# Fused two-block transformer forward on one core: the later modulation moved from TensorE to VectorE, its last eight slots beside the mixing output

## The reference, cut to what matters

```python
mod = (c_act @ w_mod + b_mod)[:, None, :]           # 2048 -> 6 * 2048, from one row c
mod_c = (cc_act @ w_mod + b_mod)[None, None, :]     # the same weights for the context row
sh1, sc1, gt1, sh2, sc2, gt2 = jnp.split(mod, 6, axis=-1)
csh1, csc1, cgt1, csh2, csc2, cgt2 = jnp.split(mod_c, 6, axis=-1)
h = rmsnorm(x, g_norm1) * (1 + sc1) + sh1           # 256 tokens
hc = rmsnorm(ctx, g_norm1) * (1 + csc1) + csh1      # 256 context tokens
# combined input projection (keys, queries, values, gates), bidirectional GLA and mLSTM scans
dec = jnp.einsum('btr,zrk->zbtk', glr, gla_w_lr) + gla_b_lr   # "z" below
gla_loga = jax.nn.log_sigmoid(dec) / 16
x = x + gt1 * merge_groups(...)                     # w_out: the mixing output
h2 = rmsnorm(x, g_norm2) * (1 + sc2) + sh2
x = x + gt2 * conv_ffn(h2, ...)                     # up, conv, down
# then a pooling block and an attention block, not touched here
```

## Time and profile before

| | |
|---|---|
| median of 3 runs | 2866.39 us (2863.33 to 2869.9) |
| the profiled execution | 2857.94 us |
| its span, first to last instruction | 2856.2 us |
| mean granted TensorE clock | 0.973 |
| PE, PEld, DVE, ACT busy | 2730.5, 2355.7, 2040.1, 1440.3 us |
| read from memory | 526.46 MB |

### The profile page before, as it was taken

How to read it: one execution, slowest core, us unless ns; L and a number is a source line. 1 busy time by engine, 2 the same in 40 slices (tenths; PEclk the granted TensorE clock), 3 DMA queues, 4 the chain that set the end, 5 groups by cost and what they waited for, 6 DMA issues and landing times.

```text
span 2856.2 us, 42600 instructions
## 1 busy us (share of the span) xinstructions
PE 2730.5 (96%) x16078; PEld 2355.7 (82%) x16078; DVE 2040.1 (71%) x3065; ACT 1440.3 (50%) x2001; POOL 0.2 (0%) x4
## 2 busy tenths in 40 slices
PE   7889999999989999999999999999999899999988
PEld 4457777998878888888888888889988898988877
DVE  6677886794778888887555777777654888556576
ACT  6544332444445555555444655554444654565563
POOL 0000000000000000000000000000000000000000
PEclk8999999999999999999999999999999899999989
DMA  9668756553245555555555455544555345433433
GB/s 346 225 238 328 273 221 236 177 183 105 75 161 177 191 191 190 185 189 187 187 192 193 164 191 186 182 175 178 184 188 191 134 164 179 175 136 108 176 135 131
DMA packets 104534, 530.21 MB, mean 186 GB/s; under 512 B 8240, under 2 KB 8784, under 8 KB 51296
## 3 DMA queue, kind: packets, MB, share of 16 engines
q1 hardware_dynamic: 103040, 524.32, 50.9%
q10 hardware_dynamic: 1376, 4.27, 0.4%
HBM read 526.46 MB, written 2.10 MB: 185 GB/s over the span
## 4 chain that ended last, share of the span: by engine, by line
PE 65%; DVE 6%; issue 3%; ACT 3%; ACTq 0%; DVEq 0%; DMA 0%
PE ps L1919 32%; PE ps L1920 16%; PE ps L1911 4%; PE ps L1913 4%; PE ps L1912 4%; DVE lo L1058 1%; ACT hi L499 1%; PE ps L2256 1%; DVE ws L1637 1%; PE ps L2425 1%; PE ps L2423 0%; PE ps L2261 0%; ACT L828 0%; ACT L499 0%; DVE R L1685 0%
## 5 line engine op out<-in xcount | busy, mean ns | idle before, releaser
L1058 DVE TENSOR_TENSOR lo<-raw,hi 128x1024 fp32r<-128x1024 f32 x700 | 845.0, 1223 | 475.4 <-ACT hi L499 471.9
L499 ACT ACTIVATE hi<-raw 128x1024 fp32r<-128x1024 f32 x700 | 732.3, 1056 | 613.7 <-PE ps L1920 545.8
L1919 PE MATMUL ps<-x,hi 128*128 128x512 f32 x1376 | 479.8, 395 | 7.3 <-DVE x L1504 7.2
L1920 PE MATMUL ps<-x,lo 128*128 128x256 f32 x1376 | 382.2, 278 | 0.0
L1919 PE MATMUL ps<-y,hi 128*128 128x512 f32 x1024 | 363.2, 399 | 3.6 <-DVE y L1889 3.6
L1919 PE MATMUL ps<-xp,hi 128*128 128x512 f32 x1024 | 361.0, 396 | 5.7 <-DVE lo L1058 3.9
L533 ACT ACTIVATE hi<-raw 128x1024 fp32r<-128x1024 f32 x194 | 200.4, 1055 | 316.3 <-PE ps L1910 137.9
L1138 DVE TENSOR_TENSOR lo<-raw,hi 128x1024 fp32r<-128x1024 f32 x194 | 230.9, 1221 | 124.6 <-ACT hi L533 124.2
L1919 PEld LDWEIGHTS ps<-x,hi 128*128 128x128 f32 x1376 | 259.0, 188 | 69.1 <-issue 8.2
L1920 PE MATMUL ps<-y,lo 128*128 128x256 f32 x1024 | 288.5, 282 | 0.0
L1920 PE MATMUL ps<-xp,lo 128*128 128x256 f32 x1024 | 287.8, 281 | 0.0
(11 more groups left out here) (384 smaller groups left out, 5075.8 us busy)
## 6 DMA issues: line engine op xcount, KB each, us to landing
raw<-in_weights SPq DMA_DIRECT2D x491, 1024.0 KB, 4.8
xf<-in_xt SPq DMA_DIRECT2D x8, 512.0 KB, 9.0
raw<-in_weights SPq DMA_DIRECT2D x4, 768.0 KB, 4.2
R<-in_xt ACTq DMA_DIRECT2D x1, 2048.0 KB, 8.1
out<-R SPq DMA_DIRECT2D x1, 2048.0 KB, 6.3
maskn<-in_maskn ACTq DMA_DIRECT2D x1, 512.0 KB, 3.7
ptr<-in_pt ACTq DMA_DIRECT2D x2, 256.0 KB, 3.8
vec<-in_vec ACTq DMA_DIRECT2D x1, 411.5 KB, 4.6
```

The source lines that it names most:

```text
L499: act.activation(HI[p % PAIR][:, c], RAW[p % RING][:, c], ACT.Copy).then_inc(hi_ready, 1)
L1058: dve.tensor_tensor(LO[p % PAIR][:, c], RAW[p % RING][:, c], HI[p % PAIR][:, c].bitcast(F32), ALU.subtract).then_inc(lo_ready, 1)
L1919: pe.matmul(o, h, pair[:, :, k, :], start=start, stop=False, **kw)
L1920: return pe.matmul(o[:, 0, :], l, pair[:, 0, k, :], start=False, stop=stop, **kw)
```

## The change

It has four parts.

1. `SUMMED` now begins with group 4: 56 slots (32 to 87) go through VectorE's multiply-and-add in the front, none of the later modulation is split. The sums of four slots go to TensorE as before, now 14 times in the front, each with its own bias addition (`later_modulation(g)`).
2. The last eight slots (88 to 95, `FINAL`) are no longer in `UNITS`: they are loaded by ScalarE's queue to two buffers of their own (`wlast`) and summed on VectorE in turns 3, 5, 6, 8, 9, 11, 12 and 14 of the mixing output; TensorE takes their two column sums behind the sum of squares.
3. The list of units is new. The slots of `MODS[3]` all stand ahead of `("key4", 2)`; behind it come `("key", 5, 0)`, the last quarter `("key4", 3)` and `("key", 5, 1)`. The operand of quarter 3 is made behind the first half of `key4 2` (`operand_made(3)`, `operand_hi(3)`, `operand_rest(3)`).
4. ScalarE makes z and |z| out of PSUM (Identity and Abs with bias), and the squares of the residual in the mixing output.

```diff
-LATER = MODS[4]
-SUMMED = [u for m in MODS[5:] for u in m]
+SUMMED = [u for m in MODS[4:] for u in m][:56]
+FINAL = [u for u in MODS[7] if u not in SUMMED]
+FINAL_TURNS = (3, 5, 6, 8, 9, 11, 12, 14)
...
-UNITS += whole(("key4", 1), ("lr_key", 0)) + modulation_of(MODS[2][6:] + MODS[3][:6]) + whole(("key4", 2))
-UNITS += modulation_of(MODS[3][6:] + LATER[:6]) + whole(("key4", 3))
...
+UNITS += whole(("key4", 1), ("lr_key", 0)) + modulation_of(MODS[2][6:] + MODS[3]) + whole(("key4", 2)) + [("key", 5, 0)]
+UNITS += whole(("key4", 3)) + [("key", 5, 1)] + modulation_of(SUMMED[:1])
+_b = 1
+for _entry in [("lr_key", 1), ("key", 6), ("key", 7)]:
+    UNITS += [(*_entry, 0)] + modulation_of(SUMMED[_b:_b + 1]) + [(*_entry, 1)] + modulation_of(SUMMED[_b + 1:_b + 2])
...
-    if _entry in (("query", 5), ("query", 7), ("gate", 1), ("gate", 3), ("gate", 6), ("gate", 8), ("gate", 11), ("gate", 13)):
+    if _entry in (("query", 4), ("query", 5), ("query", 7), ("gate", 1), ("gate", 2), ("gate", 4), ("gate", 5), ("gate", 7), ("gate", 8), ("gate", 10),
+                  ("gate", 11), ("gate", 12), ("gate", 13)):
...
+            def operand_hi(r):
+
+                for s in range(2):
+                    act.wait_ge(sem("operand_made"), reached("made", "x1", 2 * r + s + 1))
+                    act.activation(xs(xh, s, r), xs(xf, s, r), ACT.Copy).then_inc(sem("operand_hi"), 1)
...
+                    if n == AT["value", 2 * m] + 1:
...
+                            act.activation(cum[:, m * 1024 + a * 512:m * 1024 + (a + 1) * 512], PS[4 + a][:, :], ACT.Identity,
+                                           bias=v("lr_b", 2 * m + a)).then_inc(sem("dec_abs"), 1)
+                            act.activation(soft[:, c], PS[4 + a][:, :], ACT.Abs, bias=v("lr_b", 2 * m + a)).then_inc(sem("dec_abs"), 1)
...
+            def n2_square(b):
+
+                act.wait_ge(evacuated, EVAC["mix_out"] + b + 1)
+                if b >= 2:
+                    act.wait_ge(sem("square_steps"), reached("steps", "n2", b - 1))
+                act.activation((tmpx, tmpx2)[b % 2][:, :], blk(R, b), ACT.Square).then_inc(sem("squares_ready"), 1)
+
+            def load_final(i):
+
+                if i >= 2:
+                    act.wait_ge(sem("mod_summed"), 4 * (NSUM + i) - 4)
+                act.dma_start(wlast[i % 2][:, :], A["weights"][MOD_AT + FINAL[i]]).then_inc(sem(f"last_loaded{i % 2}"), 16)
...
             for u in range(16):
                 split("mix_out", u // RING, u % RING)
+                if u - 1 in FINAL_TURNS[:6]:
+                    load_final(FINAL_TURNS.index(u - 1) + 2)
                 if u:
+                    n2_square(u - 1)
                     n2_gain(u - 1)
...
+            def later_modulation(g):
+
+                dve.wait_ge(sem("sums_taken"), g + 1)
+                j = 32 + 4 * g
+                dve.tensor_tensor(mview[:, j:j + 4, 0], PS[7][:, 4 * g:4 * g + 4], v("b_mod", j, 4), ALU.add).then_inc(sem("mods_ready"), 1)
...
+            for u in range(16):
+                split("mix_out", u // RING, u % RING)
...
-                accumulate(Steps(dve, sem("square_steps"), reached("steps", "n2") + 2 * u), blk(R, u), tmpx)
+                if u:
+                    n2_sum(u - 1)
+                if u in FINAL_TURNS:
+                    i = FINAL_TURNS.index(u)
+                    dve.wait_ge(sem(f"last_loaded{i % 2}"), 16 * (i // 2 + 1))
+                    multiplied_sum(NSUM + i, FINAL[i], wlast[i % 2], range(4))
+            n2_sum(15)
...
+                if AT[kind, k] - 1 in LAST and half == (kind != "key4"):
+                    turn_rows(LAST.index(AT[kind, k] - 1))
...
             sum_squares("n2", "steps")
+            column_sums(14)
+            column_sums(15)
```

More of the change, by code:

```diff
@@ L405, in sums_of @@
         def sums_of(g):
-            return wsum[g % 2 + (0 if GROUP_ENDS[g] < AT["value", 10] else 2)]
+            return wsum[4 + g % 2 if g >= len(GROUP_ENDS) else g % 2 + (0 if GROUP_ENDS[g] < AT["value", 10] else 2)]
         def cum_of(d, c):
@@ L556, in _ @@
                 n = AT[kind, k]
-                if half and n in LAST[:5]:
+                if half and n in LAST:
                     r = LAST.index(n)
@@ L562, in _ @@
                     act.activation(mrows[:, :], PS[6 + r % 2][0:16, :], ACT.Copy).then_inc(sem("mod_rows"), 1)
+                if (kind, k, half) == ("key4", 2, 1):
+                    operand_hi(3)
                 if UNITS[u] in HALF:
@@ L587, in _ @@
                     act.wait_ge(halves_used, HALF[UNITS[u]] + 1)
-                    key_out(k, k - 5)
+                    key_out(k, 6 if k == 5 else k - 5)
                 if kind == "query":
@@ L1227, in scan, with operand_made, operand_rest @@
                 own.wait()
+            def operand_made(r):
+                modulation(r)
+                for s in range(2):
+                    gains(s, 16, s, "g1", 4 * r, 4)
+                own.wait()
+                for s in range(2):
+                    for b in range(4 * r, 4 * r + 4):
+                        f = s * KD + b
+                        ins = dve.tensor_scalar(blk(xf, f), blk(xf, f), amod[:, f:f + 1], mview[:, b, s:s + 1], ALU.mult, ALU.add)
+                    ins.then_inc(sem("operand_made"), 1)
+            def operand_rest(r):
+                for s in range(2):
+                    dve.wait_ge(sem("operand_hi"), reached("hi", "x1", 2 * r + s + 1))
+                    dve.tensor_tensor(xs(xl, s, r), xs(xf, s, r), xs(xh, s, r).bitcast(F32), ALU.subtract).then_inc(sem("operand_rest"), 1)
             dve.memset(ones[:, :], 1.0).then_inc(sem("ones_ready"), 1)
@@ L1249, in _ @@
                     level_arg(m)
+                if (kind, k, half) == ("key4", 2, 1):
+                    operand_made(3)
+                    operand_rest(3)
                 if UNITS[u] in HALF:
@@ L1286, in _ @@
                     z = cum[:, m * 1024:(m + 1) * 1024]
-                    if n == AT["value", 2 * m] + 1:
-                        for a in range(2):
-                            dve.wait_ge(sem("dec_z"), 2 * m + a + 1)
-                            own.done(dve.tensor_scalar(z[:, a * 512:(a + 1) * 512], PS[4 + a][:, :], v("lr_b", 2 * m + a), None, ALU.add))
-                        own.wait()
-                        dve.scalar_tensor_tensor(soft[:, :], z, -1.0, z, ALU.mult, ALU.max).then_inc(sem("dec_abs"), 1)
                     if n == AT["value", 2 * m + 1] + 1:
```

165 lines of the change are left out of this document (76 added, 89 removed).

## The result

The changed kernel took 2838.91 us, median of four runs (2821.49 to 2842.42), the kernel before 2867.91 (2863.33 to 2869.9). The ratio is 0.9895, 95% interval 0.9855 to 0.9935: 29 us faster, or 1%. The profiled execution took 2836.49 us, its span 2834.7. The forecast was 2830.6. Its direction and its outer range (2821 to 2846) held, its own narrower range (2823 to 2837) missed by 2 us. One of its sentences was wrong by 9 us, and some 3 us more than forecast, won elsewhere, hid a part of that; 2 us of these are granted clock and not the change.

The account below looks back on a forecast made before the run. TensorE, busy 2730 of 2856 us, was taken as the bound. Terms 45.1 - 0.95 - 5.0 - 1.7 - 1.6 = 35.8 us won, off the 2866.4 median, gave 2830.6; own range 2823 to 2837, outer 2821 to 2846.

Parts of the forecast that it names:

- Front: Up to the first value slot: it starts at 252.3 instead of 295.4 us, 43.1 won, 45.1 with clock given back.
- the rival of a front that gives back: Keys and queries: late transfers or low parts cost four waits, 8 us, leaving 28 won, 2839 us; chance 0.11.
- the 1.2 taken: Front, from `key4 2` to the first value slot: 1.2 us counted for the clock.
- Values: Value stage: three more sums, 9 us of VectorE, hide in its idle time; one more group of column sums costs 0.95.
- the sum: Whole kernel: 45.1 - 0.95 - 5.0 - 1.7 - 1.6 = 35.8 us won.
- The walk: Gates: VectorE's order followed gate by gate gives 6.7 us of TensorE waits ahead of scores; stage ends 5.0 us later.
- VectorE as the bound to the full price of 12.1 us: Rival for gates and mixing output: they lose 12.1 and 12 us, leaving 20 won, 2846 us; chance 0.13.
- The pairs: Mixing output: sums in consecutive turns (5, 6; 8, 9; 11, 12) make waits of 0.6 us each, 1.7 in all.
- The tail: End of mixing output: TensorE's wait ahead of the n2 sum is 5.9 us instead of 4.24, costing 1.6.
- the two queues: Rival in mixing output: eight transfers on ScalarE's queue compete with weights, 23 us if none hid, 2854 us; chance 0.05.
- the slower rival: Mixing output: VectorE waits for late `wlast` loads; at 19 us a load, 42 lost, 2873 us; chance 0.03.
- The last two column sums and their bias are beside the norm.: Behind the mixing output: these were taken as hidden beside the norm, with no cost in the sum.

Follow-up runs that it names:

- a0: The changed kernel run once more with no edit; 2835.13 us, ratio 0.9907.
- e7: On top of e1, four of the gates' sums moved to value slots where VectorE was idle, some value sums shifted; 2822.14 us, ratio 0.9849.
- e6: The changed kernel with no half of key quarter 5 ahead of `key4 3`, both halves behind it; 2835.93 us, ratio 0.9879.
- e9: The same kernel as e7 run once more; 2814.41 us, ratio 0.9828.
- e2: The changed kernel with four modulation sums moved from the gates into value slots 8, 10, 12 and 14; 2844.01 us, ratio 0.9919.
- e4: The kernel before with only z and |z| of the decay moved to ScalarE; 2864.52 us, ratio 0.9992.
- e5: The kernel before with only the squares of n2 moved to ScalarE; 2863.33 us, ratio 0.9984.
- e10: As e7, with the eight sums beside the mixing output in turns 1, 3, 4, 6, 8, 9, 11 and 13; 2825.15 us.
- e1: The changed kernel with both last column sums placed ahead of both bias additions; 2828.07 us, ratio 0.987.

## Why the prediction was right, and where it was wrong

**Front.** Right. `key4 2` at 158.33 (158.0 forecast), `key4 3` at 177.3 without a wait (177.6; operand at 173.3, margin 4.0 instead of 5.5), first value slot at 251.18 (252.3). No wait for `raw` in the queries, so the rival of a front that gives back is out. The clock cost 1.7 us for the 1.2 taken (granted 0.77 from 157.7 to 165.0 us, 7.3 x 0.23). The 1.2 was the author's estimate and no run shows it: behind the same wait of 2.40 us the runs showed 1.7 us by that clock, as in a0 and e7, or nothing (1.00 over the same 7.3 us, e6 and e9). (1.75 slots of 1.05 MB at 361 GB/s are 5.1 us and not 4.9; it changes nothing.)

**Values.** Right within what can be told: the sum has 2.0 us of clock back and 0.95 lost, 1.05 us won (the 2.0 are 7 x 0.28, by the 0.72 granted behind the wait of 3.50 us; the changed kernel has 1.00 over the 7.2 us from 251.0), and first value slot to first gate took 245.4 us (246.5 in a0) for 245.9, in a stage that differs by over 1 us between executions. The reason was too coarse: the three sums were hidden, four more in the same stage were not (e2), since slots 9 to 12 have no room left. A new wait of 1.8 us for a bias addition was not in the sum; those for V fell from 11.9 to 10.4.

**Gates.** The walk forecast waits of 6.7 us for `qk` (its seven terms add up to 6.8) and the trace has 5.5, ahead of the scores of the very gates it named: 0.3, 0.2, 0.1, 1.3, 1.0, 1.4 and 1.3 us at 2, 5, 7, 8, 11, 12 and 13, forecast 0.4, 1.1, 0.1, 1.6, 0.4, 1.6 and 1.6. The stage is 6.3 us longer than before where 5.0 were forecast; 4.3 are waits and 0.95 the column sums, about 1 us is open. Mechanism shown by e2 and e7: with six sums the waits are 1.0. VectorE as the bound to the full price of 12.1 us is out.

**Mixing output.** Off in size. The pairs were 1.7 us in the sum and cost 0.1 at most, with no wait. The additions behind a pair end 5.0 to 5.4 us after the slot's end, where the prediction had 6.1, so the bank was free just in time: at 758.76, for TensorE's slot 9 at 758.90, a margin of 0.14 us, where every turn of before had 2.1. The stage is 1.1 us longer, 0.85 of it in its first slot (7.31 us for 6.46, granted clock 0.75 for 0.86). That is not the change's doing: the same slot took 7.60 us in e4, which has the mixing output of before, and 6.33 in e2, which has the changed one. The tail was 1.6 us in the sum and is 0.9, for the reason given (VectorE's queue; e5, e10); ScalarE's square, 0.5 in the sum, took 0.40 us. No wait for `wlast`: its loads landed in 4.8 us (median), so neither the two queues nor the slower rival came about.

**The step that failed** is "The last two column sums and their bias are beside the norm." They were put down at nothing; they cost 9.0 us (e1). TensorE's side was looked at (0.95 us a group, with a wait for x2 to hide in) and the bias's duration (0.15 us), but not that the second group of sums waits for the first group's bias, and that this stands on VectorE behind 14 us of x2. Up to the n2 sum 38.5 us were won where the sum had 35.8. Of the 2.7 more, 2.0 are the granted clock between the gates and the mixing output, for which the sum has no term: that is luck. Without the missed 9.0 the median would have been near 2830, which is the forecast, and with it it is 2838.9. How near the medians come is luck in part too, since each is of four executions and those of the changed kernel are 21 us apart.

## What to carry to other kernels

A tiny instruction is as late as the queue it stands in (here 0.15 us of bias behind 14 us of x2, 12.93 us of waiting): for each edit "beside" something, write down what its waits need and what is ahead of that on its engine. A stage's mean idle share is no room (VectorE idled 42.5 of 155 us in the values before, but 0.8 of 20 around slots 10 and 11 of the changed kernel); look at windows of a slot or two before moving work in. Before a gain of 1 or 2 us is put down to an edit, look at the granted clock of that stretch in both profiles (0.93 and 0.96 were 2.0 us apart here). And compare waits and starts inside the profiles, not two totals, when stages can run at two periods, as here at 346.7 and 353.3 ns a pair.

## What the runs showed of the hardware

A stretch of matmul pairs (512 and 256 columns) at a granted clock of 1.00, with no wait, ran at one of two periods, 346.7 or 353.3 ns, and kept it to the end of a stage in most cases: 1376 pairs of `up` would be 9.2 us apart by that, and the stage was 7.4 and 7.9 us longer in the changed kernel's first profile than before and in a0. It differs between two executions of the same program. It can change inside a stage: in a0_again the first slots of the mixing output took 5.55 us each, one 5.74, and all behind it 5.65. What sets it wasn't found.

The other surprise is the clock behind a wait: 2.40 us of waiting ahead of `key4 2` were followed by a granted clock of 0.77 over 7.3 us in one execution (e7_spread) and of 1.00 in another of the same program (e9_spread_again), 1.7 us apart by these clocks.
